# Keys of both partition halves written by ScalarE instead of by SBUF to SBUF transfers

## What is computed

```python
qa = rms_norm(to_heads(sb_q, SB_HEADS, SB_HEAD_DIM), sb_q_g)
ka = rms_norm(to_heads(sb_k, SB_HEADS, SB_HEAD_DIM), sb_k_g)
# for each block of 128 queries, over the keys up to it
z = jnp.einsum('bhqd,bhkd->bhqk', qb, kb) * scale
log_keep = jnp.where(valid, jax.nn.log_sigmoid(-z), 0.0)
later = lax.cumsum(log_keep, axis=3, reverse=True) - log_keep
w = jnp.where(valid, jnp.exp(jax.nn.log_sigmoid(z) + later), 0.0)
outs.append(jnp.einsum('bhqk,bhkd->bhqd', w, vb))
```

## Time and profile before

| | us |
|---|---|
| median of 3 runs | 1067.2 |
| lowest and highest | 1065.8 and 1068.86 |
| the profiled execution, its time | 1068.55 |
| its span, first to last instruction | 1066.7 |

### The profile page before, as it was taken

The page is one execution under the profiler, slowest core; times in us unless marked ns, Lnnn a source line. Parts: engine busy times, 40 slices in busy tenths (PEclk is TensorE's granted clock), DMA queues, the critical chain, the costliest instruction groups (busy, mean ns, idle before and its releaser), DMA issues.

```text
span 1066.7 us, 14151 instructions
## 1 busy us (share of the span) xinstructions
PE 982.7 (92%) x5739; PEld 821.0 (77%) x5739; DVE 544.1 (51%) x806; ACT 310.6 (29%) x709; POOL 205.8 (19%) x100
## 2 busy tenths in 40 slices
PE   3699989689999899999799996999999879999998
PEld 3589989467777788887677885888887768787886
DVE  4876893498777345443133155133334663844522
ACT  7432011358777322123511010123322402111000
POOL 0001110250000021212121111101101354774000
PEclk9799999679999999999999997999999989999999
DMA  9671400601110212122112535212113934345331
GB/s 297 183 200 59 141 1 1 200 3 39 36 38 17 60 45 54 40 60 60 50 40 95 152 90 123 75 41 70 41 58 92 344 99 154 122 158 177 100 99 60
DMA packets 119051, 100.57 MB, mean 94 GB/s; under 512 B 18024, under 2 KB 98497, under 8 KB 118731
## 3 DMA queue, kind: packets, MB, share of 16 engines
q1 hardware_dynamic: 118986, 99.67, 30.9%
HBM read 73.44 MB, written 24.12 MB: 91 GB/s over the span
## 4 chain that ended last, share of the span: by engine, by line
PE 68%; DVE 15%; DMA 9%; ACT 3%; issue 2%; POOL 2%; SPq 1%; ACTq 0%; DVEq 0%
PE psum L726 32%; PE psum L264 5%; PE psum L265 5%; PE psum L266 5%; PE psum L940 4%; DMA sg<-z_scratch 3%; PE psum L925 3%; DMA w3raw<-in_w_in 2%; PE psum L911 2%; DVE macc L486 2%; DVE ohi L1763 1%; PE psum L1254 1%; PE psum L913 1%; DVE blocks L1587 1%; DVE gacc L486 1%
## 5 line engine op out<-in xcount | busy, mean ns | idle before, releaser
L726 PE MATMUL psum<-hhi,w3hl 128*128 128x512 f32 x1152 | 387.4, 407 | 22.2 <-issue 19.5
L726 PEld LDWEIGHTS psum<-hhi,w3hl 128*128 128x128 f32 x1152 | 221.6, 192 | 72.8 <-issue 24.4
L726 PE MATMUL psum<-hlo,w3hl 128*128 128x512 f32 x576 | 228.7, 397 | 0.0
L716 POOL TENSOR_TENSOR w3hl<-w3raw,w3hl 128x1024 fp32r<-128x1024 f32 x44 | 107.5, 2444 | 529.9 <-DVE w3hl L710 529.9
L726 PEld LDWEIGHTS psum<-hlo,w3hl 128*128 128x128 f32 x576 | 111.1, 193 | 23.1 <-issue 2.2
L710 DVE CAST w3hl<-w3raw 128x1024 fp32r<-128x1024 f32 x44 | 35.9, 815 | 154.1 <-DMA w3raw<-in_w_in 134.0
L264 PE MATMUL psum<-w1hi,hhi 128*128 128x256 f32 (+2 forms) x320 | 100.9, 315 | 9.0 <-DVE hlo L449 5.6
L1031 DVE TENSOR_TENSOR_SCAN stick<-stick,zero 128x1024 f32<-128x1024 f32 (+7 forms) x64 | 91.8, 1472 | 18.7 <-ACT stick L983 18.6
L265 PE MATMUL psum<-w1lo,hhi 128*128 128x256 f32 (+2 forms) x320 | 99.6, 311 | 0.0
L266 PE MATMUL psum<-w1hi,hlo 128*128 128x256 f32 (+2 forms) x320 | 99.6, 311 | 0.0
L784 ACT COPY zst<-psum 128x512 f32<-128x512 f32 x48 | 28.2, 588 | 189.6 <-PE psum L726 189.6
(11 more groups left out here) (212 smaller groups left out, 1412.9 us busy)
## 6 DMA issues: line engine op xcount, KB each, us to landing
w3raw<-in_w_in SPq DMA_DIRECT2D x36, 512.0 KB, 4.2
z_scratch<-zst SPq DMA_DIRECT2D x48, 256.0 KB, 2.2
ada<-in_ada_w SPq DMA_DIRECT2D x16, 512.0 KB, 5.3
sg<-z_scratch SPq DMA_DIRECT2D x8, 1024.0 KB, 4.8
xrow<-in_x SPq DMA_DIRECT2D x4, 1024.0 KB, 8.1
w1raw<-in_w_in SPq DMA_DIRECT2D x4, 1024.0 KB, 7.1
adag<-in_ada_w SPq DMA_DIRECT2D x8, 512.0 KB, 4.2
zraw<-z_scratch SPq DMA_DIRECT2D x8, 512.0 KB, 7.5
```

The source lines that it names most:

```text
L716: nc.gpsimd.tensor_tensor(w3lo[:, i % 2], w3raw[:], cast(w3hi[:, i % 2]), ALU.subtract).then_inc(w3_lo, 1)
L726: t = nc.tensor.matmul(out_, a[:, i % 2, kt, :], moving[b][:, kt, 512 * half:512 * half + 512], start=(ends[0] and kt == k0 and m == 0), s ...
```

## The change

ScalarE's `high(u)` makes four copies in a key turn: for each head one to partitions 0 to 63 and one to partitions 64 to 127, both from the same PSUM bank. It gives `fh_ok` after the last. In a query turn it makes two, as before. `second_half` and its transfers are gone, and so are the semaphore `dup_ok` and TensorE's wait for it.

```diff
         def sp_2(sp):
             sp.dma_start(v_dram[1:1 + S].rearrange("(t p) n -> p t n", p=P), rows[:, 2]).then_inc(vd_out, 16)
             sp.dma_start(mraw[:], const_v[:, 4]).then_inc(c2_in, 16)
-            def second_half(u):
-
-                pp, _, cols = half_of(u)
-                sp.wait_ge(fh_ok, u + 1)
-                sp.dma_start(cast(qk[HD:P, pp, 1, :, cols]), cast(qk[0:HD, pp, 1, :, cols])).then_inc(dup_ok, 16)
-
-            for u in range(2):
-                second_half(u)
             sp.wait_ge(vd_out, 32)
...
             for n in range(NST + 5):
-                u = turn_at(n)
-                if u is not None and u % 4 < 2:
-                    second_half(u)
                 m = (n - 5) // 2
...
                 if n % PER == 0:
                     pe.wait_ge(fl_ok, 4 * pair + 3)
-                    pe.wait_ge(dup_ok, 32 * (pair + 1))
...
                 for head in range(2):
-                    t = nc.scalar.copy(qk[0:HD, pp, part, head, cols], turn_bank(u)[HD * head:HD * head + HD])
+                    for rows_ in (slice(0, HD), slice(HD, P))[:1 + part]:
+                        t = nc.scalar.copy(qk[rows_, pp, part, head, cols], turn_bank(u)[HD * head:HD * head + HD])
                 t.then_inc(fh_ok, 1)
```

More of the change, by code:

```diff
@@ L829, in turn_at @@
             return 4 * (n // PER + 1) + k if 0 <= k < 4 and n // PER + 1 < PAIRS else None
-        (c2_in, c2_ok, v_in, e_in, dv_ok, ve_mm, ve_ok, z_mm, keep_ok, scan_ok, q_mm, fh_ok, fl_ok, dup_ok, t_mm, w_ok,
+        (c2_in, c2_ok, v_in, e_in, dv_ok, ve_mm, ve_ok, z_mm, keep_ok, scan_ok, q_mm, fh_ok, fl_ok, t_mm, w_ok,
          v_mm, o_ok) = (sem("a_" + n) for n in (
              "c2_in", "c2_ok", "v_in", "e_in", "dv_ok", "ve_mm", "ve_ok", "z_mm", "keep_ok", "scan_ok", "q_mm", "fh_ok",
-             "fl_ok", "dup_ok", "t_mm", "w_ok", "v_mm", "o_ok"))
+             "fl_ok", "t_mm", "w_ok", "v_mm", "o_ok"))
         o_out = [sem(f"a_o_out{i}") for i in range(2)]
```

## The result

| | before | changed |
|---|---|---|
| median of 10 runs, us | 1066.78 | 1072.22 |
| lowest to highest | 1064.21 to 1068.99 | 1069.3 to 1075.08 |
| profiled execution, span | 1066.7 | 1070.5 |

The ratio is 1.0051, with a 95% interval of 1.0035 to 1.0067. The change makes the kernel 5.4 us slower (3.7 to 7.1). I had predicted 6.4 us slower, 1073.6 us.

What follows compares the result with a forecast made beforehand. The prediction took TensorE as the bound, with ScalarE close behind. Groups +7.1 us and head transfers -0.7 us gave +6.4 us on a median of 1067.2: 1073.6 us, range 1069.5 to 1077.0.

Steps and rivals of the forecast that it cites:

- The head as no bottleneck: Head of attention: a wait for the mask's cast replaces TensorE's 6.58 us wait, ends 0.3 us later and costs nothing.
- The price of a copy: ScalarE's added copies: 0.595 us each with the small gap; 16 new ones make 9.5 us of ScalarE.
- The first key turn: In each group: `fh_ok` comes 1.19 us later, delaying VectorE's `low` and TensorE's second turn; full cost 1.19 us.
- The second key turn: In each group: its copies aren't hidden, so ScalarE and then TensorE run 2.38 us late; three groups give +7.1 us.
- from 243.45 to 250.4 ScalarE has no other idle time: ScalarE's queue in the first group: no slack there, so everything after the second key turn is 2.38 us late.
- The clock: Rival, 0.06: TensorE's clock falls behind group waits grown to 2.1 us, about 1.7 us more a group; 1075.3 to 1078.8.
- The transfers' own worth: Head: removing two 256 KB transfers spares `vsh` its slow start, so `w3raw` lands earlier; -0.7 us, bounds 0 to 2.5.
- the first pair runs in a gap: Head: the two transfers mostly run after `v_scratch` has landed, before data of `vE`, `vsh` and `w3raw` are there.

Runs made afterwards that it cites:

- E3: Kernel before, with four ScalarE copies only in each group's first key turn; the second and the head keep transfers. Ratio 1.006 (1.0037 to 1.0083).
- E1: Kernel before, with four ScalarE copies in the key turns of the three groups only; the head keeps its transfers. Ratio 1.0072, 7.7 us slower.
- E11: Changed kernel, with VectorE's rounding of `w3raw` moved from ahead of the first scan to behind scan 59. Median 1062.70 us, ratio 0.9978 to the kernel before.
- E2: Kernel before, with four ScalarE copies and no transfers at the head only; the groups keep transfers. Ratio 0.9982 (0.9966 to 0.9998), 1.9 us faster.
- E4: Changed kernel, with `fh_ok` given after the two lower copies; upper copies follow from SBUF with their own semaphore. Ratio 1.0019 to the kernel before.
- E5: Changed kernel, with TensorE's second turn of a group waiting for the VectorE step two turns back, not one. Ratio 1.0007 to the kernel before.
- E6: Changed kernel, with 12 extra transposes on TensorE ahead of the second turn's wait in each group. Ratio 1.0073 to the kernel before.
- E7: Kernel before, with VectorE's rounding of `w3raw` and its wait moved from ahead of the first scan to behind scan 59. Median 1055.19 us, ratio 0.9922.
- E12: Kernel before, with two more head transfers of the same size and form, for which TensorE also waits. Ratio 1.0029 (1.0013 to 1.0044), 3.1 us slower.
- E8: Kernel before, with `w3raw`'s rounding behind scan 59 and pair 0's keys copied by ScalarE without transfers. Median 1054.29 us, ratio 0.9913.
- E10: As E9, with pair 0's keys copied by ScalarE without transfers at the head. Median 1052.10 us, ratio 0.9875 to the kernel before.
- E9: Kernel before, with `w3raw`'s rounding behind scan 59 and TensorE's second turn not waiting for the VectorE step just ahead. Median 1052.31 us, ratio 0.9883.

## Why the prediction was right

**The head as no bottleneck: right.** TensorE's 6.58 us wait for a transfer looked like the prize. It went, and a wait of 6.94 us for the cast took its place. From the issue of `v_scratch` TensorE started 10.64 us on (192.18 to 202.82), before 10.28, so 0.36 us later where I had worked out 0.3. The chain stayed on `w3raw`.

**The price of a copy: right.** 48 copies at 0.580 us, 2.35 us for four. The Trainium skill's page "ScalarE: Activation LUTs", section "What ACT_TABLE_LOAD costs", gives 520 ns from start to start by its formula. For this form that is too low: the trace has 595 ns, in the changed kernel too.

**The first key turn: right.** 1.19 us predicted, 1.18 measured in E3 alone, and it goes by the path that I named (VectorE's wait 3.40, TensorE's 2.08).

**The second key turn: right in kind, a little too large.** The step "from 243.45 to 250.4 ScalarE has no other idle time" is the one that failed. It gave 1.19 us, the runs show 0.91. A timeline gives each instruction from start to end, and those of ScalarE overlap, so short waits between them don't appear as idle time. They can be found by the starts: from `keep` at 245.46 to the next copy at 245.89 it was 0.43 us before, and 0.26 us (247.53 to 247.79) after. With `copy_out` to `keep` (0.33 and 0.26) that makes 0.24 us of the 0.28 that are missing in a group. A group costs 2.09 us at full clock, three cost 6.3, not 7.1.

**The clock: a rival at 0.06 that took place, at a smaller price.** I kept it out of the sum. In the changed kernel's profile it happened in two of three groups, in E1 in two, in E3 and E11 in one each; with waits of 0.90 us and less (before, E2, E4, E5, E6, E7) in none. I priced it at 1.7 us a group. It cost 0.66 and 0.7 in the changed kernel and 1.6 in E3. The timelines suggest why: in the changed kernel ScalarE sets the pace behind the second key turn and hides part of TensorE's slower work, while in E3 ScalarE itself waits for TensorE there, 0.93 and 0.47 us. One row that I had set the rival against was misread: the pause that ends at 663.9 is 4.18 us long in the timeline and not "over 3", so the waits between which 2.1 lay were 1.3 and 4.2. The Trainium skill's page "TensorE: Matmul & The Clock Gate", Part 1, ties the half rate to idle time. The trace agrees in kind, and shows it for a wait of 2.08 us in 6 groups and not in 6 others.

**The transfers' own worth: sized too large in the trace, open in the time.** The term of 0.7 us counted the slow start of `vsh` as the transfers' doing. By the profiles it is 0.2 to 0.5 us at the first scan, and nothing is left of it at the first group (47.71 against 47.72 us). E12's second pair, which costs all of its 2.5 us, fits the reason I gave (the first pair runs in a gap). Two comparisons of medians (E2 against before, E1 against the changed kernel) give about 2 us instead, two others (E8 against E7, E10 against E9) 0.9 and 0.2 us. It may be that without the transfers `w3raw` lands soon more often, or that the clock rises early more often, as in E2's profile; both would matter in the first two only. Five profiles without and three with them are too few to say. That stays open.

So the sum of the stage is 3 x 2.09 + 0.66 + 0.7 + 0.0 = 7.6 us, as measured in the profile, against 5.4 (3.7 to 7.1) in the medians. My 6.4 lies between, in part by luck: the slack that I overlooked (-0.8), the falls of the clock that I left out (up to +1.4) and the head (+0.7 in the trace, -1.2 by E2's median) pull in both directions. Why the medians show 2 us less than the profile isn't shown.

## What to carry to other kernels

A long wait in front of an engine isn't a cost until the chain goes through it: here 6.6 us of waiting were worth next to nothing, and a wait for weights that were needed some 140 us later was worth 8 us. Work moved from a transfer to a compute engine has to be placed in that engine's queue, instruction by instruction, and the idle time beside it counts only if the moved work isn't what causes it. Before a wait is filled or lengthened, look whether its semaphore is needed at all: the change of one index in a wait gave 1.1 us for each group, for nothing.

## What the runs showed of the hardware

- TensorE's granted clock fell from 1.00 to 0.50 behind a wait of 2.08 us in 6 of 12 groups, and in none of those with 0.90 us or less. Twelve transposes in the wait kept it up.
- The price of such a fall was 0.66 to 0.7 us where ScalarE set the pace, and 1.6 us in E3, where TensorE did.
- In the head the clock rose to 1.00 at 228 in the profiles of before and changed and between 219 and 220 in that of E2; two stretches of matmuls took 3.66 us at 0.50 and 2.00 us at 1.00.
- A scan of 1024 elements took 2.29 us alone and 4.42 us beside GpSimd's subtractions, and a subtraction 2.35 us alone and 4.34 beside scans. Each then takes about as long as one of both kinds in a row (4.64 us). A landing of `w3raw` that came 1.3 us later moved the first scan by 2.4 us.
- The load of 512 KB for `w3raw` took between 10.0 and 11.9 us to land from one execution to the next, with the same transfers ahead of it.
- Transfers from 64 partitions to the other 64 move 209 to 211 GB/s with all DMA engines busy, about half of the 403 to 407 GB/s of the load behind them.
